# Turning round the time-step product, grouping the prefix sums and splitting the scan's wait in a hybrid decoder layer

## What is computed

```python
proj = x @ w_in                                   # T x (...), dt_raw is 32 of its columns
xbc_c, cv_new = causal_depthwise_conv(xbc, cv_prev, w_ssd_conv)
xbc_c = jax.nn.silu(xbc_c + b_ssd_conv)           # 2048 columns xs, 512 bm, 512 cm
dt = jax.nn.softplus(dt_raw + dt_bias)            # one time step for each token and head
a = -jnp.exp(a_log)
...
def step(h, inp):                                 # over chunks of 128 tokens
    acs = jnp.cumsum(da_c, axis=1)                # da = dt * a: the prefix sums
    lmat = jnp.exp(where(causal, acs[t] - acs[s], -inf))
    y = einsum(c_c, b_c) * lmat @ xdt_c + (c_c @ h) * exp(acs)
    h_new = h * exp(acs[-1]) + b_c @ (xdt_c * exp(acs[-1] - acs))
```

## Time and profile before

| | us |
|---|---|
| median of three runs | 1797.49 |
| lowest and highest | 1796.89, 1803.19 |
| the profiled execution, with what lies around its span | 1800.88 |
| its span, from the first to the last instruction | 1799.1 |
| PE busy in it | 1712.4 (95%) |
| DVE, ACT, POOL busy | 1185.8, 904.1, 110.6 |

### The profile page before, as it was taken

The page is one execution under the profiler, slowest core; times in us unless marked ns, Lnnn a source line. Parts: engine busy times, 40 slices in busy tenths (PEclk is TensorE's granted clock), DMA queues, the critical chain, the costliest instruction groups (busy, mean ns, idle before and its releaser), DMA issues. The chain is left out here.

```text
span 1799.1 us, 30135 instructions
## 1 busy us (share of the span) xinstructions
PE 1712.4 (95%) x10798; PEld 1490.3 (83%) x10799; DVE 1185.8 (66%) x1520; ACT 904.1 (50%) x1273; POOL 110.6 (6%) x234
## 2 busy tenths in 40 slices
PE   7999899999999999999999899599999999999996
PEld 7999899999867999999787687477888888888872
DVE  5466667667566542223443346689999999999984
ACT  4333544443312632223333331378888888888870
POOL 0000000000000000000000000011111111111110
PEclk9899999999999999999999999699999999999997
DMA  5122454443465222432654444389999999999954
GB/s 198 38 82 83 115 152 125 146 144 108 152 221 176 83 83 86 165 119 89 196 184 169 194 158 175 126 313 341 370 357 375 378 382 391 382 377 357 365 214 150
DMA packets 133220, 374.11 MB, mean 208 GB/s; under 512 B 22544, under 2 KB 45712, under 8 KB 130416
## 3 DMA queue, kind: packets, MB, share of 16 engines
q1 hardware_dynamic: 123632, 363.99, 56.5%
q0 software_dynamic: 9504, 8.94, 1.5%
HBM read 360.33 MB, written 38.22 MB: 222 GB/s over the span
## 5 line engine op out<-in xcount | busy, mean ns | idle before, releaser
L2192 DVE TENSOR_TENSOR wl<-eraw,wh 128x1024 fp32r<-128x1024 f32 x396 | 471.9, 1222 | 29.4 <-ACT wh L1398 7.4
L1398 ACT ACTIVATE wh<-eraw 128x1024 fp32r<-128x1024 f32 x396 | 416.9, 1063 | 88.2 <-PE ps L1031 69.6
L1589 DVE TENSOR_TENSOR wl<-raw,wh 128x1024 fp32r<-128x1024 f32 x152 | 184.7, 1222 | 180.6 <-ACT wh L1108 180.3
L606 PE MATMUL ps<-xh,wh 128*128 128x272 f32 x1136 | 246.7, 299 | 5.4 <-DVE wl L1589 5.4
L606 PE MATMUL ps<-xh,wl 128*128 128x272 f32 x1136 | 236.6, 290 | 0.0
L606 PE MATMUL ps<-xl,wh 128*128 128x272 f32 x1136 | 236.3, 290 | 0.0
L1031 PE MATMUL ps<-wh,xgh 128*128 128x512 f32 x528 | 210.6, 399 | 4.7 <-DVE xgl L2197 3.2
L1031 PE MATMUL ps<-wl,xgh 128*128 128x512 f32 x528 | 207.5, 393 | 0.0
L1031 PE MATMUL ps<-wh,xgl 128*128 128x512 f32 x528 | 207.1, 392 | 0.0
L606 PEld LDWEIGHTS ps<-xh,wh 128*128 128x128 f32 x1136 | 181.6, 191 | 16.1 <-issue 12.8
L606 PEld LDWEIGHTS ps<-xl,wh 128*128 128x128 f32 x1136 | 180.7, 191 | 0.0
(11 more groups left out here) (384 smaller groups left out, 2860.6 us busy)
## 6 DMA issues: line engine op xcount, KB each, us to landing
eraw<-in_w SPq DMA_DIRECT2D x396, 512.0 KB, 5.8
raw<-in_slabs SPq DMA_DIRECT2D x152, 512.0 KB, 4.2
bc<-acs_dram SPq DMA_DIRECT2D x16, 512.0 KB, 6.6
hs<-in_h SPq DMA_DIRECT2D x16, 512.0 KB, 3.6
out_h_sample<-hs SPq DMA_DIRECT2D x16, 512.0 KB, 3.2
kv<-in_kT SPq DMA_DIRECT2D x8, 1024.0 KB, 5.2
kv<-in_vc SPq DMA_DIRECT2D x4, 1024.0 KB, 7.7
kvx<-in_vc SPq DMA_DIRECT2D x2, 2048.0 KB, 11.1
```

Source lines behind the costliest of these rows:

```text
L606: r = nc.tensor.matmul(ps[:, 2 * (ub % 2) + half, 0:HT], w[:, s, col], x[:, koff + kk, half * HT:half * HT + HT], start=first and kk == 0 ...
L1398: nc.scalar.activation(wh[:, b % RING], eraw[:, slot], ACT.Copy).then_inc(w_hi, 1)
L1589: v.tensor_tensor(wl[:, s], raw[:, s], wh[:, s].bitcast(F32), ALU.subtract).then_inc(w_lo, 1)
L2192: v.tensor_tensor(wl[:, b % RING], eraw[:, (b - DENSE) % ERAW], wh[:, b % RING].bitcast(F32), ALU.subtract).then_inc(w_lo, 1)
```

## The change

Three things.

1. The time-step product stands behind slab 2 instead of slab 3, with the operands exchanged: wdt is the weights, 32 columns wide, xraw streams past it, 272 tokens at a time. Depth tiles 0 and 4 write partitions 0 to 31, 1 and 5 partitions 32 to 63, and so on (`at_`), so that four partial sums lie above each other. ACT copies them to SBUF (`dpart`). Behind slab 3 five products with dpart as weights against four stacked identities (a ninth tile of wdt) add the four and turn them back, with tokens on the partitions. dt_mm and dt_a count one more.
2. The prefix sums of the four chunks are made in one product of 128 columns for each of the three matrices, instead of one of 32 columns for each chunk and matrix; the four transposed sums follow each other, then the samples' own.
3. The wait for all convolutions before the scan is gone; the first step of each group waits for B, C and the four tiles of its own group.

```diff
-        wdt = place("wdt", [P, KT, HEADS], F32, t0 + 4896)
+        wdt = place("wdt", [P, KT + 1, HEADS], F32, t0 + 15392)
+        dpart = place("dpart", [P, T], F32, t0 + 13216)
...
             first_unit()
-            for m in range(1, 4):
+            for m in range(1, 3):
                 slab_unit(m, m, xh, xl)
 
             pe.wait_ge(in_sem["dt"], 48)
+            for half in range(2):
+                for kk in range(KT):
+                    at_ = HEADS * (kk % 4)
+                    r = nc.tensor.matmul(ps[at_:at_ + HEADS, 4 + half, 0:HT], wdt[:, kk], xraw[:, kk, half * HT:half * HT + HT],
+                                         start=kk < 4, stop=kk >= 4)
+            r.then_inc(dt_mm, 1)
+            slab_unit(3, 3, xh, xl)
+
+            pe.wait_ge(dt_a, 1)
             for t in range(TT):
-                for kk in range(KT):
-                    r = nc.tensor.matmul(ps[:, 4, HEADS * t:HEADS * t + HEADS], xraw[:, kk, t * P:t * P + P], wdt[:, kk],
-                                         start=kk == 0, stop=kk == KT - 1)
+                n_ = P if t < CHUNKS else SAMP
+                r = nc.tensor.matmul(ps[0:n_, 4, HEADS * t:HEADS * t + HEADS], dpart[:, t * P:t * P + n_],
+                                     wdt[:, KT], start=True, stop=True)
             r.then_inc(dt_mm, 1)
             for m in range(4, 6):
                 slab_unit(m, m, xh, xl)
...
-            for t in range(TT):
-                n_ = P if t < CHUNKS else SAMP
-                da = da_tok[0:n_, t]
-                nc.tensor.matmul(ps[0:n_, 5, HEADS * t:HEADS * t + HEADS], tri if t < CHUNKS else tri_s, da, start=True, stop=True)
-                nc.tensor.matmul(ps[0:n_, 6, HEADS * t:HEADS * t + HEADS], suf if t < CHUNKS else suf_s, da, start=True, stop=True)
-                if t < CHUNKS:
-                    nc.tensor.matmul(ps[:, 7, HEADS * t:HEADS * t + HEADS], ones, da, start=True, stop=True)
-                    nc.tensor.matmul(ps[0:HEADS, 4, t * P:t * P + P], da, tri, start=True, stop=True)
-                else:
-                    nc.tensor.matmul(ps[0:HEADS, 5, 256:256 + n_], da, tri_s, start=True, stop=True)
+            da, da_s, own = da_tok[:, 0:CHUNKS].rearrange("p c h -> p (c h)"), da_tok[0:SAMP, CHUNKS], HEADS * CHUNKS
+            nc.tensor.matmul(ps[:, 5, 0:own], tri, da, start=True, stop=True)
+            nc.tensor.matmul(ps[:, 6, 0:own], suf, da, start=True, stop=True)
+            nc.tensor.matmul(ps[:, 7, 0:own], ones, da, start=True, stop=True)
+            for t in range(CHUNKS):
+                nc.tensor.matmul(ps[0:HEADS, 4, t * P:t * P + P], da_tok[:, t], tri, start=True, stop=True)
+            nc.tensor.matmul(ps[0:SAMP, 5, own:own + HEADS], tri_s, da_s, start=True, stop=True)
+            nc.tensor.matmul(ps[0:SAMP, 6, own:own + HEADS], suf_s, da_s, start=True, stop=True)
+            nc.tensor.matmul(ps[0:HEADS, 5, 256:256 + SAMP], da_s, tri_s, start=True, stop=True)
...
-            pe.wait_ge(dt_a, 3)
-            pe.wait_ge(silu_done, 2 + CT)
+            pe.wait_ge(dt_a, 4)
             for it in range(STEPS):
                 g, c = divmod(it, CHUNKS)
...
+                if c == 0:
+                    pe.wait_ge(silu_done, 2 + 2 * GROUPS + GT * (g + 1))
...
-            for m in range(4):
+            for m in range(3):
                 conv_in(m, BC, 0)
+            act.wait_ge(dt_mm, 1)
+            nc.scalar.activation(dpart[:].rearrange("p (h t) -> p h t", h=2), ps[:, 4:6, 0:HT], ACT.Copy).then_inc(dt_a, 1)
+            conv_in(3, BC, 0)
```

More of the change, by code:

```diff
@@ L1157, in _ @@
             conv_in(5, BC, 0)
-            act.wait_ge(dt_mm, 2)
+            act.wait_ge(dt_mm, 3)
             nc.scalar.activation(dte_tok[:, 0:CHUNKS], ps[:, 6, 0:CHUNKS * HEADS].rearrange("p (c h) -> p c h", h=HEADS), ACT.Exp)
@@ L1604, in steps @@
             def steps():
-                dve.wait_ge(dt_mm, 1)
+                dve.wait_ge(dt_mm, 2)
                 dve.wait_ge(in_sem["dt"], 48)
@@ L1612, in steps @@
                 v.scalar_tensor_tensor(sp[:, 0], sp[:, 5], -1.0, sp[:, 5], ALU.mult, ALU.max).then_inc(dt_v1, 1)
-                dve.wait_ge(dt_a, 1)
+                dve.wait_ge(dt_a, 2)
                 v.tensor_scalar(sp[:, 2], sp[:, 1], 1.0, None, ALU.add).then_inc(dt_v1, 1)
-                dve.wait_ge(dt_a, 2)
+                dve.wait_ge(dt_a, 3)
                 dve.wait_ge(dt_v1, 2)
@@ L1634, in sums @@
             def sums():
-                dve.wait_ge(dt_mm, 2)
+                dve.wait_ge(dt_mm, 3)
                 v.tensor_copy(acs_tok[:, 0:CHUNKS], ps[:, 5, 0:CHUNKS * HEADS].rearrange("p (c h) -> p c h", h=HEADS))
@@ L2359 @@
     ins = {
-        "xT": cols(x.T), "cst": cst, "slabs": np.stack(stream), "wdt": cols(w[:, o_dt:o_dt + HEADS]),
+        "xT": cols(x.T), "cst": cst, "slabs": np.stack(stream), "wdt": np.concatenate([cols(w[:, o_dt:o_dt + HEADS]), np.tile(np.eye(HEADS, dtype=np.float32), (P // HEADS, 1))[:, None]], 1),
         "dt_bias": I["ssd_dt_bias"], "a_log": I["ssd_a_log"], "d_skip": I["ssd_d"].reshape(XT, 2).T,
```

## The result

| | before | changed |
|---|---|---|
| median of five runs, us | 1801.54 | 1788.89 |
| lowest and highest | 1796.89, 1803.19 | 1788.20, 1790.04 |
| span of the profiled execution | 1799.1 | 1787.5 |

The ratio on record is 0.9936, with a 95% interval from 0.9919 to 0.9952, so the kernel is faster by 0.64%. The forecast was 15.4 us and 1782.1; the time lies 0.4 us above the range. The first three runs of before, on which the forecast's base rested, had a median of 1797.49, 4 us under that of all five.

What follows compares the result with a forecast made beforehand. PE, busy 95% of 1799.1 us, was taken as the path. Gains of 12.1 and 5.8 less losses of 1.0 and 1.5 gave 15.4 us, from the median 1797.49 to 1782.1; range 1777.0 to 1788.5.

Steps and rivals of the forecast that it cites:

- Part 1: Time-step product: 13.6 us removed, 2.1 and 1.2 added, 1.8 of clock gained, together 12.1 us gained, bounds 10.0 to 12.3.
- the clock's 1.8: Behind the old time-step product: 3.92 us at clock 0.53 cost 1.8 us, taken as gained; at worst nothing of it.
- Part 2: Prefix sums between slabs 5 and 6: 6.60 us become 2.6, and 1.8 of slow clock behind goes; 5.8 us gained.
- What is late next: DVE's chain behind the shortened product: new PE wait of 0.7 us at slab 6, 0.3 at slab 8; 1.0 us lost.
- the forecast's last paragraph: Signs in the profile: clock 1.00 from 13 us to the scan, slab 23 16.9 us earlier, Mt wait about 7.5 us.
- Part 3: Scan step 0: a 7.5 us wait for Mt replaces 6.0, half clock behind costs 2.7; net loss 1.5 us.
- The step that failed: PE's stream after the front: a microsecond removed there should reach the end, so the summed 15.4 us arrive whole.
- A: Time-step product: column sets don't overlap or their loads stand open; costs 3.4 to 6.3 us, 1785.5 to 1788.4; chance 8%.
- B: Shortened stretches in front: the clock falls all the same, 1.8 us behind and up to 1.3 in it; chance 15%.
- C: Scan's new wait: no slow stretch follows, so the split wait gains 1.2 us, giving 1779.4; chance 8%.
- D: Scan step 0: the clock stays low after the longer idle; through group 0 it costs 31 us, 1813; chance 2%.

Runs made afterwards that it cites:

- e9: The changed kernel without the split convolution wait and with the old prefix sums, so the new time-step product alone: median 1787.61 against 1799.64, ratio 0.9939.
- e6: The changed kernel with all 16 time-step products on one column set instead of four: median 1794.51, ratio 0.9966 to the kernel before.
- e5: The kernel before with only the grouped prefix sums added: median 1795.76, ratio 0.9973.
- e7: The kernel before run again, nothing changed: median 1800.56, ratio 1.0004.
- e3: The kernel before with only the convolution wait split by group: median 1803.26, ratio 1.0006.
- e8: The kernel before with only the input wdt enlarged by the ninth tile, loaded but never used: median 1801.14, ratio 1.0004.
- e1: The changed kernel run again, nothing changed: median 1790.47 against 1802.47 for the kernel before, ratio 0.9929.
- e12: The kernel of e11 plus 16 unread products of 128x272 behind slab 7, a filler of 2.0 us: median 1788.63, ratio 0.9939 to the kernel before.
- e2: The changed kernel with the wait for all 24 convolutions before the scan put back: median 1785.84, ratio 0.9905 to the kernel before.
- e11: The kernel of e2 run again on another chip: median 1786.08, ratio 0.9925 to the kernel before.
- e4: The changed kernel with bc loaded ahead of the wait for the last convolution rows and step 0's Relu ahead of the last silu: median 1783.42, ratio 0.989.
- e10: The kernel of e4 with the wait for all 24 convolutions before the scan put back: median 1787.68, ratio 0.9931 to the kernel before.

## Why the prediction was right and wrong

**Part 1** was right in its terms: 2.04 us for the product (2.1), 1.08 from 38.92 to 40.00 for the turning-back (1.2), the copy in its cover (it ended at 36.70, PE asked at 38.9), and the clock's 1.8. Alone it brought more than its 12.1, 15.1 us at slab 23 in e9, as the clock held through the old sums too. The rule of the Trainium skill (TensorE: Matmul & The Clock Gate, "Part 3: Packing small matmuls"), that loads overlap only in another row group, would have given 5.5 us. The trace differs: the 32 loads of 106 to 110 ns each lie within 2.04 us, and e6 shows that the four sets share the time. The measurement decides.

**Part 2** was right in its place: 2.66 us measured in e5 for 2.6, and the slow stretch behind it gone. That its 5.8 us add to part 1's was not borne out: behind part 1 it was worth 1.3 to 1.6 us at slab 23. The forecast counted 3.3 us of clock in and behind the old sums as theirs (6.60 x 0.23 and 1.8); the clock fell there in the kernel before, e7 and e3, and held in e8 and e9, so they come and go with the execution. That the total at slab 23 came out so near is in part luck: part 1 brought what part 2 didn't.

**What is late next** was right in kind and a little large: a wait of 0.47 us for low half 6 instead of 0.7. At slab 23 the forecast was 16.9 us ahead; measured 16.4, and 15.3 in e1, where the clock fell at slab 2, which the forecast's last paragraph had excluded from 20 us on.

**Part 3** was right in mechanism and sign. There was a wait of 7.65 us (7.5) for Mt, the products for Mt started 1.3 us earlier (1.2), and the half clock behind them lasted 4.0 us and cost 2.0 (2.7). The net loss was 0.7 us for 1.5, then 1.0 in e1, 1.2 in e3 and 1.3 in e6, with 4.8 to 5.4 us of half clock. What I had not seen is the other side of the comparison: behind the old 6.0 us wait the half clock is no fixed price either. It lasted 6.1 us in the kernel before, 5.3 to 5.5 in e9 and e12, and 3.2 in e2 and e11; in those two the clock had fallen 2.3 to 2.4 us into the wait and in the others 4.4 to 5.3. Against e2 and e11 part 3 costs about 2 us at this place, against e12 it would be about 1, and in the medians it is 1 to 4.6. On the kernel before (e3) it is 0.8 in the median, within the noise.

**The step that failed** is the sentence that a microsecond taken out of PE's stream in front should reach the end, and that no later wait runs by its own time. 15.7 us were there at the scan (forecast 15.4) and 11.6 at the end. The waits for al and kv are DMA waits of 2.2 and 3.9 us in the list of before, and both got longer (3.7 and 5.1), and the half-clock stretch behind two waits doubled, from 3.4 to 6.8 us. They do not simply run by their own time, or they would have grown by all of the 15 us: the load of ah itself took 9.7 us from issue to landing instead of 8.2. The rows were in the trace; the prediction named the waits only up to 200 us and put the clock elsewhere at 1.8 us in the range, with no term. Even in front its list was not whole: the longest wait there, 8.4 us for the first slab's low half, is missing, though the change leaves it as it was (8.5).

How much is handed back between step 1 and the end differs: 4.1 and 4.4 us in the two profiles of the changed kernel, 3.1 and 0.2 in the two of parts 1 and 2, 5.2 in e4, and between 0.9 and 4.6 in the other kernels (e3, e5, e6, e8, e9, e10, e12). The mean of the twelve is 2.6, and for the kernel before again it was nothing. A term of that size would have put the forecast at 12.8 us, and 12.65 were measured; but it is known only afterwards, and the mean takes in e3 and e8, whose edits gain nothing in front, so the near hit says little.

**The larger part of the miss** in the absolute time is not this step but the base. The miss is 6.8 us (1788.89 for 1782.1). The median of before was 1797.49 over three runs and 1801.54 over five, which is 4.05 of it; counted from 1801.54, the 15.4 us give 1786.1, and 2.75 us are left for the step that failed.

Of the rivals, A fell with e6 and the 2.04 us. B did not happen in the changed kernel (but the clock fell at slab 2 in e1, e2 and e5, where no rival had it). C and D did not: behind the long wait for Mt there was half clock in each of the four profiles, for 4.0 us in the changed kernel's first and for 4.8 to 5.4 us in e1, e3 and e6, and then the clock was back at 1.00.

**Still open.** What decides how long the half clock behind one and the same wait lasts. And why the loads of ah take 9.4 to 10.1 us in all kernels with part 1 or 2, and 8.2 to 8.7 in the kernel before, with part 3 alone and with the larger input alone. The size of the input is excluded (e8); whether it is what else is in flight when they are issued wasn't tried.

## What to carry to other kernels

A wait that ends at the same instant as before, because its chain hangs on another queue, only changes its name when the wait ahead of it is loosened; look for the chain that ends next and shorten it in the same edit, as e4 did for 7 us against the changed kernel (2.4 us against leaving the wait alone). The idle stretches of PE of 4.2, 6.0 and 7.7 us cost their length and a slow clock behind them, while the 2.66 us of e4 cost only their length in its profile. Work that used to run at half clock in the shadow of another wait must be priced again when it moves. Read the list of waits to the end of the kernel before you let a gain in front pass through 1600 us of it, and don't take a clock stretch of one profile as the property of one edit: repeat the kernel before first.

## What the runs showed of the hardware

Four products of 32 columns each, on four column sets, run in the time of one and a bit: 2.04 us against 7.52 us for the same 16 products on one set. The clock stayed at 1.00 through 7.5 us of products that use only 32 of 128 columns, with 272 columns streaming (e6), but was 0.63 through 13.6 us of full-width weights against 32 columns. Through the old prefix sums it was 0.77 in the kernel before and 1.00 in e8 and e9. Waits of 2.6 us near 900 us had a half-clock stretch at their end in some profiles (the kernel before, the changed one) and none in others (e1, e2). The same wait of 4.19 us for yl is followed by a half-clock stretch of 3.4 us in the kernel before, e6, e7, e9 and e12, and of 6.8 in the changed kernel, e1 to e5, e8, e10 and e11, counted with the part that lies in the wait.
